# A norm weight spread over 128 partitions: by a DMA through a DRAM row in place of matmuls against the identity

## The reference, cut to what matters

```python
mod_lat = split(silu(c) @ ada_w + ada_b, 6)
g_pre, g_post, g_pre_ff, g_post_ff = norm_gains
...
h_lat = h_lat + mod_lat[2] * rmsnorm(y_lat, g_post)
f_lat = square(relu(modulate(rmsnorm(h_lat, g_pre_ff), mod_lat[3], mod_lat[4]) @ mlp_w_in)) @ mlp_w_out
h_lat = h_lat + mod_lat[5] * rmsnorm(f_lat, g_post_ff)
```

## Time and profile before

| | |
|---|---|
| median of 3 runs | 761.62 us (759.96 to 761.80) |
| profiled execution | 759.97 us, of which the span of instructions 758.30 us |
| PE busy | 746.5 us, 98% |
| DVE busy | 549.5 us, 72% |
| ACT busy | 363.8 us, 48% |
| POOL busy | 10.7 us, 1% |
| granted TensorE clock | full in all 40 slices of the span |
| DMA | 152.18 MB, 201 GB/s over the span |

### The profile page before, as it was taken

One profiled execution on the slowest core, in us unless ns is written; L12 is line 12 of the kernel. 1 busy time (PEld: TensorE's weight loads), 2 busy tenths in 40 slices (PEclk: granted clock), 3 DMA queues, 4 the chain that ended last, 5 costly groups with the idle time before them and its releaser, 6 DMA issues.

```text
span 758.3 us, 13288 instructions
## 1 busy us (share of the span) xinstructions
PE 746.5 (98%) x5378; PEld 694.2 (92%) x5378; DVE 549.5 (72%) x782; ACT 363.8 (48%) x450; POOL 10.7 (1%) x27
## 2 busy tenths in 40 slices
PE   6999999999999999999999999999999999999998
PEld 6789965999998888899979999999999999999998
DVE  5677998856556743558899976849879988887441
ACT  4116332754554333375554546584557555554330
POOL 0000000000000000020000001000000000000000
PEclk9999999999999999999999999999999999999999
DMA  9999998365566974436445153336563655433640
GB/s 276 304 334 388 380 356 320 129 224 187 166 192 215 343 235 179 167 125 223 150 145 196 70 194 124 123 129 231 200 222 112 222 173 188 175 122 130 210 141 29
DMA packets 61728, 152.18 MB, mean 201 GB/s; under 512 B 2992, under 2 KB 42288, under 8 KB 51440
## 3 DMA queue, kind: packets, MB, share of 16 engines
q1 hardware_dynamic: 61312, 150.20, 57.9%
q0 software_dynamic: 368, 1.31, 0.5%
HBM read 150.45 MB, written 1.05 MB: 200 GB/s over the span
## 4 chain that ended last, share of the span: by engine, by line
PE 94%; SPq 3%; DMA 1%; DVE 1%; ACT 1%; issue 0%; ACTq 0%
PE ps L1421 21%; PE ps L1423 21%; PE ps L1422 21%; PE ps L1498 4%; PE ps L1578 4%; PE ps L1577 4%; PE ps L1576 4%; PE ps L1623 4%; SPq L396 2%; DMA keyed_odd<-in_w_sc_in 1%; PE ps L1712 1%; PE ps L1711 1%; PE ps L1710 1%; PE ps L1438 1%; PE ps L1563 1%; PE ps L1561 1%
## 5 line engine op out<-in xcount | busy, mean ns | idle before, releaser
L889 DVE TENSOR_TENSOR w_lo<-raw,w_hi 128x2048 fp32r<-128x2048 f32 (+2 forms) x116 | 246.0, 2123 | 91.5 <-ACT w_hi L522 91.3
L1421 PE MATMUL ps<-a_hi,w_hi 128*128 128x256 f32 x1056 | 299.9, 284 | 0.0
L1423 PE MATMUL ps<-a_hi,w_lo 128*128 128x256 f32 x1056 | 297.8, 282 | 0.0
L1422 PE MATMUL ps<-a_lo,w_hi 128*128 128x256 f32 x1056 | 297.4, 282 | 0.0
L522 ACT ACTIVATE w_hi<-raw 128x2048 fp32r<-128x2048 f32 (+2 forms) x116 | 205.8, 1777 | 100.6 <-PE ps L1578 45.9
L1421 PEld LDWEIGHTS ps<-a_hi,w_hi 128*128 128x128 f32 x1056 | 198.7, 188 | 1.3 <-issue 0.7
L1422 PEld LDWEIGHTS ps<-a_lo,w_hi 128*128 128x128 f32 x1056 | 199.2, 189 | 0.6 <-issue 0.5
L1423 PEld LDWEIGHTS ps<-a_hi,w_lo 128*128 128x128 f32 x1056 | 198.7, 188 | 0.0
L1421 PE MATMUL ps<-up_hi,w_hi 128*128 128x256 f32 x192 | 54.7, 285 | 0.0
L1422 PE MATMUL ps<-up_lo,w_hi 128*128 128x256 f32 x192 | 54.2, 282 | 0.0
L1423 PE MATMUL ps<-up_hi,w_lo 128*128 128x256 f32 x192 | 53.8, 280 | 0.0
(11 more groups left out here) (254 smaller groups left out, 918.5 us busy)
## 6 DMA issues: line engine op xcount, KB each, us to landing
raw<-in_w_z_in SPq DMA_DIRECT2D x26, 1024.0 KB, 4.8
raw<-in_w_up SPq DMA_DIRECT2D x22, 1024.0 KB, 4.8
raw<-in_w_mlp_in SPq DMA_DIRECT2D x16, 1024.0 KB, 4.8
raw<-in_w_mlp_out SPq DMA_DIRECT2D x16, 1024.0 KB, 5.6
raw<-in_w_down SPq DMA_DIRECT2D x16, 704.0 KB, 4.0
raw<-in_ada SPq DMA_DIRECT2D x32, 256.0 KB, 6.3
raw<-in_ada_half SPq DMA_DIRECT2D x8, 1024.0 KB, 7.1
raw<-in_ada SPq DMA_DIRECT2D x8, 1024.0 KB, 7.0
```

The lines of the kernel that those rows point to most:

```text
L889: e.tensor_tensor(w_lo[:, slot, 0:words], raw[:, unit_slot, 0:words], w_hi[:, slot, 0:words].bitcast(f32), SUB).then_inc(raw_used, 1)
L1421: e.matmul(dst, w_hi[:, slot, cols], hi, start=start, stop=False, skip_group_check=skip)
L1422: e.matmul(dst, w_hi[:, slot, cols], lo, start=False, stop=False, skip_group_check=skip)
L1423: return e.matmul(dst, w_lo[:, slot, cols], hi, start=False, stop=stop, skip_group_check=skip)
```

## The change

PE's widening after block 12, DVE's two copies and PE's wait for them are taken out. A DRAM tensor `gain_row` of 1 by 1024 is added. POOL waits for the columns, writes them to the row in DRAM by one DMA (each of the 1024 elements of 4 bytes to its own place), waits until that has landed, and reads the row back to all 128 partitions of `hid` by a second DMA. DVE waits for that one ahead of its first `post_ff` chain. The first norm weight keeps its widening on PE.

```diff
+        gain_row_out = sem("gain_row_out")
+        gain_row_in = sem("gain_row_in")
+        gain_row = nc.dram_tensor("gain_row", (1, D), f32).ap()
...
             constant(e.memset(sc_cv[:, :, :], 0.0), 4)
+
+            e.wait_ge(gain_cols, 2)
+            e.dma_start(gain_row.rearrange("o (i p) -> p (o i)", p=P), gain_post_ff[:, :],
+                        allow_slow_non_contiguous=True).then_inc(gain_row_out, 16)
+            e.wait_ge(gain_row_out, 16)
+            e.dma_start(flat(hid[:, :, :]), gain_row.broadcast_to([P, D])).then_inc(gain_row_in, 16)
 
             e.wait_ge(w_used, USED + FIRST["z_in"])
...
                     e.tensor_tensor(gain_post_ff[:, :], mod[:, 40:48], pcol("gains", 24, 8), MUL).then_inc(gain_cols, 1)
-                if j == 13:
-                    gain_evict(gain_ff_b, 1)
+            e.wait_ge(gain_row_in, 16)
             token_chain("post_ff", 0, gain_ff_b, x_t, y_t)
...
-                if j == 12:
-                    widen(gain_post_ff, 1)
...
             turn_back(0)
-            e.wait_ge(gain_in, 4)
             turn("post_ff", 0, y_t)
```

## The result

The changed kernel takes 762.46 us in the median of 11 runs (760.11 to 764.73), the kernel before 760.22 us in 11 runs taken beside it (759.88 to 761.80). The ratio is 1.0028, with a 95% interval of 1.0020 to 1.0037: 0.28% slower, about 2.1 us. It lies within 0.3%, but on the other side of before than the forecast of 0.23% less.

What follows compares the result with a forecast made beforehand. PE was taken to bound the kernel, busy 98% of the span. Removing the widening gave -1.78 us and all other terms 0, so 761.62 - 1.78 = 759.8 us, 0.23% less, range 757.6 to 763.0.

Steps and rivals of the forecast that it cites:

- What bounds the kernel: Whole kernel: PE, busy 98% of the span; an edit is worth what it takes from or adds to PE's queue.
- the first term: PE's queue between blocks 12 and 13: removing the widening of gain_post_ff gives back 1.78 us in full.
- The cover: From gain_post_ff written to DVE's first read of the row: 19.02 us plus about 1.0 us slack hides the transfers.
- the cost of the two transfers: POOL's write and read back of the row: 13.0 us, bounds 5.8 and 23.3, hidden, so term 0.
- the high bound of 23.3: Both transfers at their dearest: write 16.1, read 7.0, POOL's waits 0.2 us.
- the write's 7.7 us: POOL's write of 1024 elements to DRAM: 1.36 to first packet, 4.4 for packets, 1.9 to land.
- the weight loads' average share, 0.47: Read back of the row: weight loads hold the engines 0.47 of the cover, so at most 7.0 us; 5.1 taken.
- My 1.9 us for landing: End of POOL's write: lands like the trace's smallest DMAs, 128 KB, 1.9 us after issue.
- an estimated 8.8 us: The write if read-modify-write below 512 B doubles engine time per element; left open, the sum unchanged.
- Rival B: DVE's wait before the first post_ff chain: the row comes too late; 763.1 to 774.5 us, chance 0.14.
- its mild end: Row ready after 23.3 us, 3.3 late at DVE's wait: +1.5 us, 763.1 us.
- The range: Whole kernel's time, to hold 8 in 10: 757.6 to 763.0 us; within 0.3% had chance 0.66.

Runs made afterwards that it cites:

- experiment 7: Changed kernel with its second DMA reading 128 different rows of 4 KB instead of one row 128 times: ratio 1.0047 to the kernel before, 763.73 us.
- experiment 6: Changed kernel with the 4-byte write issued from ACT's queue, the read still from POOL: ratio 1.0040 to the kernel before, 763.50 us.

## Why the prediction was wrong

**What bounds the kernel, and the first term.** Right. The widening stood in PE's queue and came out of it: from `gain_post_ff` to the end of the last `mlp_out` matmul it is 25.47 us where it was 27.25, 1.78 less, and no weight load took it back.

**The cover.** Right in kind and size. I had the first read of the row at 316.4 us with lateness counting from 20.0 us after the columns. In the changed kernel, 0.6 us later in all, the row would have been read at about 317.0 and was read at 320.36: 3.4 us late, of which 2.09 reached PE, so that the slack was 1.3 where I had 1.0.

**The step that failed** is the cost of the two transfers, "7.7 + 5.1 + 0.2 = 13.0 us". They took 11.8 + 9.7 and 0.9 us between (0.6 from the columns to the first issue, 0.3 to the second), 22.4 us, close to the high bound of 23.3. Both were mis-sized for one reason, and it was not the one I weighed. Of the write's 7.7 us I had given 1.36 + 4.4 = 5.8 to issue and packets and 1.9 to landing. The first part was too dear: the last recorded packet was through 3.8 us after the issue, POOL's queue was held for 1.08 us and not 4.4, and from ACT's queue an element held an engine for 9 ns and not 43. The term that failed is the landing: 7.9 us from the last packet to the end instead of 1.9, and until after that the same engines moved weight loads at a fraction of their pace. With space between the elements the landing is some 0.6 us and the whole write 4.7. That made the second transfer slow as well: I had bounded it by the weight loads' average share, 0.47, at 7.0 us, and it met two loads held up together, 9.7 us.

My 1.9 us for landing, from 128 KB stores, was the wrong row to lean on: no row showed small neighbouring writes at all. The rule of the Trainium skill cited there (DMA: Bandwidth & Descriptors, Specifications) pointed the right way, to a dearer write, but not at the size or the cause: I took the read, modify and write as a doubling of each packet, an estimated 8.8 us. With separate places the write took 4.7 us, though every element there is as small; so it is not the size under 512 B alone that is slow.

**Rival B** is what happened, at its mild end, with the mechanism named (DVE's wait, released by the DMA) but with 0.14. Its mild price was +1.5 us, from 3.3 us of lateness; measured are about +2.1. It lacked the clock, 1.6 us in the profiled run, which makes up for a lateness that was smaller than I priced: 22.4 is 2.4 beyond 20.0, and 2.09 of it reached PE. The clock's term was missing from every case: I asked what a longer wait of PE costs in time and not what it does to the clock when PE has nothing to do.

**The range** of 757.6 to 763.0 held the median of the changed kernel, 762.46, and the change lies within 0.3%, which had 0.66. That it held is luck: it was built on a median of 761.62 from three runs, and the kernel before took 760.22 in 11. Moved down by these 1.4 us it ends at 761.6 and misses. And the whole interval of the ratio is on the slower side, where the forecast was a gain.

**What stays open.** Why neighbouring small writes land so late and hold the engines was not settled, only that it takes DRAM and neighbours. The clock fell after 3.07 us of idle PE in the changed kernel, and after 3.92 in experiment 7, and stayed full after 3.06 in experiment 6; what decides between them is open.

## What to carry to other kernels

A transfer off the critical path is worth nothing until its end is compared with the moment its reader wants it, and a write and the read behind it have to be priced by a row of the trace that has their shape, not their size; where there is none, the range has to say so. Here a vector stored across partitions was cheap to write to DRAM in runs (32 bytes: 4.3 us, but in another order, which the reader must then want) or to places apart (4.7 us; reading them back was not tried), and dear element by element into neighbouring words (12 us, and the loads behind it held up). And where a hand-off is a few us late, look first whether its start can be moved up: two edits of an index turned 0.28% of loss into 0.28% of gain.

## What the runs showed of the hardware

- A DMA of 1024 4-byte elements into 4 KB of DRAM took 11.3 to 12.1 us from POOL and 14.8 from ACT; into places 512 bytes apart 4.7; into SBUF 4.6; as 128 runs of 32 bytes 4.3; 512 elements into 2 KB 11.4.
- Such a write's last recorded packet was through 3.8 us after the issue, and the write landed 7.9 us later; with places 512 bytes apart it landed some 0.6 us after its last packet. Until about 2.7 us past the landing, packets of weight loads held an engine for 1.1 us instead of 0.31, and the 1 MB load issued before the landing took 10.0 to 11.2 us instead of 4.8.
- The granted TensorE clock fell to half after an idle stretch of 3.07 us and made 16 matmuls take 3.22 us instead of 2.05. In another run it stayed full after 3.06 us.
- POOL's mask of 128 by 1024 (1.09 us) and a DVE multiplication by a column, starting 0.01 us before it, got in each other's way: DVE's ended 0.08 us after POOL's, 1.18 us instead of 0.28. The same happened in a second run (0.02 us before it, 1.19 us).
